# mLSTM stage of a diffusion step: decay and weight rows by transfer, mask by a minimum, two numerator banks, one gate product

## The reference

```python
b = cumsum(log_sigmoid(forget gate)); dmat = where(causal, b_t - b_s + i_s, -inf)
m_t = max(b_t + m, max_s dmat)
s   = (q @ k.T) * exp(dmat - m_t)
num = exp(b + m - m_t) * (q @ C) + s @ v
den = exp(b + m - m_t) * (q @ n) + sum(s)
h   = num / max(|den|, exp(-m_t))
```

## Time and profile before

| | us |
|---|---|
| median of 3 runs | 1567.22 (1565.61 to 1571.27) |
| the profiled execution | 1569.15 |
| its span, first to last instruction | 1567.5 |

### The profile page before, as it was taken

One profiled execution on the slowest core, in us unless ns is written; L12 is line 12 of the kernel. 1 busy time (PEld: TensorE's weight loads), 2 busy tenths in 40 slices (PEclk: granted clock), 3 DMA queues, 4 the chain that ended last, 5 costly groups with the idle time before them and its releaser, 6 DMA issues.

```text
span 1567.5 us, 21088 instructions
## 1 busy us (share of the span) xinstructions
PE 1424.5 (91%) x7059; PEld 1167.0 (74%) x7059; DVE 920.4 (59%) x1259; ACT 733.7 (47%) x1127; POOL 155.9 (10%) x174
## 2 busy tenths in 40 slices
PE   6999888999999899999969879999999999999960
PEld 2766478999999789976638767888888877888750
DVE  1325558433333682216654598555555999999967
ACT  1333545332222433313342466445445888888851
POOL 1000004300000050002200071000000000000013
PEclk9899989999999999989979799999999999999985
DMA  9785652964444245225545399666665999999922
GB/s 329 254 281 178 244 180 72 357 186 131 127 130 121 67 103 140 80 89 184 164 148 170 121 367 374 212 188 198 218 187 182 373 382 375 383 374 374 381 90 86
DMA packets 253682, 336.95 MB, mean 215 GB/s; under 512 B 16670, under 2 KB 210460, under 8 KB 253484
## 3 DMA queue, kind: packets, MB, share of 16 engines
q1 hardware_dynamic: 241210, 299.55, 58.3%
q0 software_dynamic: 11120, 36.43, 6.2%
q10 hardware_dynamic: 1282, 0.04, 0.0%
HBM read 313.41 MB, written 21.50 MB: 214 GB/s over the span
## 4 chain that ended last, share of the span: by engine, by line
PE 81%; DVE 9%; ACT 3%; DMA 3%; issue 3%; SPq 1%; POOL 0%; DVEq 0%; ACTq 0%; POOLq 0%
PE PS L2006 23%; PE PS L479 14%; PE PS L2013 11%; PE PS L468 6%; PE PS L469 6%; PE PS L470 6%; PE PS L598 2%; DVE wlo L1871 2%; DVE wlo L454 1%; PE PS L1356 1%; PE PS L623 1%; PE PS L1981 1%; DMA raw<-in_ada_w 1%; DVE X L773 1%; DVE BIG L768 1%
## 5 line engine op out<-in xcount | busy, mean ns | idle before, releaser
L454 DVE TENSOR_TENSOR wlo<-raw,whi 128x1024 fp32r<-128x1024 f32 x130 | 172.1, 1350 | 252.2 <-ACT whi L451 251.8
L1871 DVE TENSOR_TENSOR wlo<-BIG,whi 128x1024 fp32r<-128x1024 f32 x192 | 238.1, 1256 | 66.6 <-ACT whi L1867 65.2
L1867 ACT ACTIVATE whi<-BIG 128x1024 fp32r<-128x1024 f32 x192 | 202.8, 1060 | 67.5 <-PE PS L2006 40.1
L2006 PE MATMUL PS<-whi,Hh 128*128 128x512 f32 x560 | 223.3, 399 | 2.3 <-DVE Hl L1928 2.2
L1871 DVE TENSOR_TENSOR wlo<-raw,whi 128x1024 fp32r<-128x1024 f32 x150 | 188.2, 1264 | 53.9 <-ACT whi L1867 52.4
L2006 PE MATMUL PS<-whi,Hl 128*128 128x512 f32 x560 | 219.1, 391 | 0.0
L2006 PE MATMUL PS<-wlo,Hh 128*128 128x512 f32 x560 | 218.9, 391 | 0.0
L468 PE MATMUL PS<-Hh,whi 128*128 128x384 f32 x608 | 206.7, 340 | 8.3 <-DVE Hl L758 6.5
L469 PE MATMUL PS<-Hl,whi 128*128 128x384 f32 x608 | 205.1, 337 | 0.0
L470 PE MATMUL PS<-Hh,wlo 128*128 128x384 f32 x608 | 204.9, 337 | 0.0
L1867 ACT ACTIVATE whi<-raw 128x1024 fp32r<-128x1024 f32 x150 | 158.5, 1059 | 70.8 <-PE PS L2013 41.0
(11 more groups left out here) (344 smaller groups left out, 1968.2 us busy)
## 6 DMA issues: line engine op xcount, KB each, us to landing
raw<-in_moe_w_gu SPq DMA_DIRECT2D x224, 256.0 KB, 5.7
BIG<-in_moe_w_gu SPq DMA_DIRECT2D x224, 256.0 KB, 6.0
raw<-in_ada_w SPq DMA_DIRECT2D x96, 512.0 KB, 4.9
BIG<-in_moe_w_down SPq DMA_DIRECT2D x80, 512.0 KB, 7.6
raw<-in_ffn_w_gu SPq DMA_DIRECT2D x44, 512.0 KB, 4.8
raw<-in_w_in_c SPq DMA_DIRECT2D x32, 512.0 KB, 3.9
raw<-in_moe_w_down SPq DMA_DIRECT2D x32, 512.0 KB, 7.3
scr_tok<-BIG POOLq DMA_DIRECT2D x29, 512.0 KB, 9.5
```

The source lines that it names most:

```text
L454: self.eng.tensor_tensor(wlo[:, s, :], raw[:, s, :], whi[:, s, :].bitcast(f32), ALU.subtract).then_inc(lo_made, 1)
L1867: act.activation(whi[:, slot(v), :], moe_raw(v), ACT.Copy).then_inc(hi_made, 1)
L1871: dve.tensor_tensor(wlo[:, slot(v), :], moe_raw(v), whi[:, slot(v), :].bitcast(f32), ALU.subtract).then_inc(lo_made, 1)
L2006: last = pe.matmul(PS[:, 6 * b + c % 2, :], lhs, wt[:, s, 512 * k:512 * k + 512], start=(q == 0 and k == 0 and lhs is h and wt is whi), st ...
```

## The change

The gate weights are put in one tile of 64 columns per block (16 input gates, 16 zeros, 16 forget gates, 16 zeros). Eight products alternate between two halves of the array's columns, and the halves are added on VectorE. In the loop TensorE no longer spreads rows: `negM` and `wint` go to DRAM once, and GpSimd's queue loads each unit's rows into `E` and `qw`, broadcast over 128 partitions. ScalarE's exponents are done in place, VectorE applies the mask by a minimum with 0 or 1, GpSimd multiplies the weight row by q. The numerator alternates between banks 2 and 3, the scores lie in another order, the transposes move to bank 4, the denominator takes two small steps for three, and the modulation units go ahead of the finished head's work.

```diff
-    masks = np.concatenate([np.where(s <= q, 0.0, BIG_NEG), np.where(s >= q, 0.0, BIG_NEG)], 1)
+    masks = np.concatenate([s <= q, s >= q], 1)
...
+        def key_blocks(e, d, key):
+
+            if key == 0:
+                return e[:, 0:128]
+            if key == 1:
+                return e.rearrange("p (a n) -> p a n", a=4)[:, 1::2, :] if d == 0 else e[:, 128:256]
+            return e[:, 256:384] if d == 0 else e[:, 256:512]
+
+        SUMS = ((((0, 0),), ((128, 1),), ((384, 1), (256, 2))),
+                (((0, 0),), ((128, 1), (384, 2)), ((256, 2),)))
...
-            for dst, w in ((4, wgi), (5, wgf)):
-                for k in range(KT):
-                    last = pe.matmul(PS[0:16, dst, 0:T], w[:, k, :], H32[:, k, :], start=(k == 0), stop=(k == KT - 1))
+            for k in range(KT):
+                at = 64 * (k % 2)
+                last = pe.matmul(PS[at:at + 64, 4, 0:T], wgp[:, k, :], H32[:, k, :], start=(k < 2), stop=(k >= KT - 2))
             last.then_inc(gates_mm, 1)
...
+                        st4 = PS[:, 0, :].rearrange("p (a n) -> p a n", a=4)
                         pe.matmul(PS[:, 0, 0:128], kM[:, h, 0:128], qM[:, h, 0:128], start=True, stop=True)
-                        pe.matmul(PS[:, 0, 128:T], kM[:, h, 128:256], qM[:, h, 128:T], start=True, stop=True)
-                        pe.matmul(PS[:, 1, 0:256], kM[:, h, 256:T], qM[:, h, 128:T], start=True, stop=True
+                        pe.matmul(st4[:, 1::2, :], kM[:, h, 128:256],
+                                  qM[:, h, 128:T].rearrange("p (a n) -> p a n", a=2), start=True, stop=True)
+                        pe.matmul(PS[:, 0, 256:384], kM[:, h, 256:T], qM[:, h, 256:T], start=True, stop=True)
+                        pe.matmul(PS[:, 1, 0:128], kM[:, h, 256:T], qM[:, h, 128:256], start=True, stop=True
                                   ).then_inc(st_made, 1)
-                    if i >= 1:
-                        pe.wait_ge(e_made, i)
-                    row = cr[0:16, 0, r:r + 1].to_broadcast([16, 128])
-                    spans = ((0, 384, 0), (384, 512, 256)) if d == 0 else ((0, 256, 0), (256, 512, 128))
-                    for lo, hi, tok in spans:
-                        for part in (nmh, nml):
-                            pe.matmul(PS[:, 2, lo:hi], row, part[:, tok:tok + hi - lo],
-                                      start=(lo == 0 and part is nmh), stop=False, skip_group_check=True)
-                    for lo in (0, 128, 384):
-                        last = pe.matmul(PS[:, 2, lo:lo + 128], cr[:, 0, :], cr[:, 1 + d, :],
-                                         start=False, stop=(lo == 384), skip_group_check=True)
-                    last.then_inc(d_made, 1)
-                    if i >= 1:
-                        pe.wait_ge(qw_made, i)
-                    pe.matmul(PS[:, 4, 0:256], row, wih, start=True, stop=False)
-                    pe.matmul(PS[:, 4, 0:256], row, wil, start=False, stop=True).then_inc(wb_made, 1)
+                        if h >= 2:
+                            pe.wait_ge(ht_made, h - 1)
+                        if h:
+                            pe.wait_ge(kw_made, h)
+                        pe.transpose(PS[:, 4, 0:128], kM[:, h, 0:128], C("ident")).then_inc(km_turned, 1)
                 if 0 <= i - 1 < NM:
                     u = i - 1
                     h, d, r = unit(u)
                     pe.wait_ge(p_done, u + 1)
+                    pe.wait_ge(qw_made, u + 1)
...
-                    if u >= 1:
-                        pe.wait_ge(rd_done, u)
+                    if u >= 2:
+                        pe.wait_ge(rd_done, u - 1)
...
+                        dst = PS[:, 2 + u % 2, 129 * t:129 * t + 129]
+                        for j, (col, key) in enumerate(SUMS[d][t]):
...
-                    if u % 2 == 1:
+                    if u:
                         pe.wait_ge(co_made, u)
-                    if u % 2 == 1 and h >= 1:
-                        pe.wait_ge(ht_made, h)
                     pe.matmul(PS[:, 7, 0:129], kw[:, d, :], V1[:, 0, h, :], start=True, stop=True).then_inc(c_made, 1)
-                if i < NM and i % 2 == 0:
-                    h = i // 2
-                    if h:
-                        pe.wait_ge(co_made, 2 * h)
-                    pe.transpose(PS[:, 7, 0:128], kM[:, h, 0:128], C("ident")).then_inc(km_turned, 1)
+                if i < NM:
+                    ada.units(2)
                 if i >= 3 and i % 2 == 1:
                     h = (i - 3) // 2
                     pe.wait_ge(hn_made, h + 1)
-                    pe.wait_ge(co_made, min(i, NM))
+                    pe.wait_ge(kw_made, min(h + 2, HM))
+                    if h:
+                        pe.wait_ge(ht_made, h)
                     for t in range(TT):
-                        last = pe.transpose(PS[:, 7, 128 * t:128 * t + 128], hn[:, t, :], C("ident"))
+                        last = pe.transpose(PS[:, 4, 128 * t:128 * t + 128], hn[:, t, :], C("ident"))
...
-            ch.step(dve.tensor_scalar(g[1], PS[0:16, 5, 0:T], bgf[:, 0:1], None, ALU.add))
+            ch.step(dve.tensor_scalar(g[1], PS[32:48, 4, 0:T], bgf[:, 0:1], None, ALU.add))
+            ch.step(dve.tensor_tensor(g[1], g[1], PS[96:112, 4, 0:T], ALU.add))
             ch.step(dve.tensor_scalar(g[2], g[1], -1.0, None, ALU.mult))
             dve.tensor_tensor(g[2], g[2], g[1], ALU.min).then_inc(nab_made, 1)
+            dve.wait_ge(gi_made, 1)
+            ch.step(dve.tensor_tensor(g[0], g[0], PS[64:80, 4, 0:T], ALU.add))
...
-                    act.wait_ge(d_made, i + 1)
-                    if i >= 2:
-                        act.wait_ge(num_made, i - 1)
-                    for t, lo, hi in KEYS[d]:
-                        last = act.activation(E[:, i % 2, lo:hi], PS[:, 2, lo:hi], ACT.Exp,
-                                              bias=nat[:, t, r:r + 1])
+                    act.wait_ge(row_in[i % 2], 48 * (i // 2 + 1))
+                    for key in range(3):
+                        e = key_blocks(E[:, i % 2, :], d, key)
+                        last = act.activation(e, e, ACT.Exp, bias=nat[:, key, r:r + 1])
                     last.then_inc(e_made, 1)
...
-                    dve.wait_ge(wb_made, i + 1)
-                    if i >= 2:
-                        dve.wait_ge(num_made, i - 1)
-                    dve.tensor_tensor(qw[:, d, :], PS[:, 4, 0:256], qM[:, h, 128:T], ALU.mult).then_inc(qw_made, 1)
-                    dve.wait_ge(st_made, h + 1)
                     dve.wait_ge(e_made, i + 1)
                     e = E[:, i % 2, :]
+                    e3 = e[:, 0:384].rearrange("p (a n) -> p a n", a=3)
+                    ch.step(dve.tensor_tensor(e3, e3, cr[:, 1 + d, :].bitcast(f32).unsqueeze(1).to_broadcast([128, 3, 128]),
+                                              ALU.min))
+                    dve.wait_ge(st_made, h + 1)
                     if d == 0:
+                        last = dve.tensor_tensor(e, e, PS[:, 0, :], ALU.mult)
+                    else:
                         dve.tensor_tensor(e[:, 0:384], e[:, 0:384], PS[:, 0, 0:384], ALU.mult)
-                        last = dve.tensor_tensor(e[:, 384:512], e[:, 384:512], PS[:, 1, 128:256], ALU.mult)
-                    else:
-                        dve.tensor_tensor(e[:, 0:256], e[:, 0:256], PS[:, 0, 0:256], ALU.mult)
-                        last = dve.tensor_tensor(e[:, 256:512], e[:, 256:512], PS[:, 1, 0:256], ALU.mult)
+                        last = dve.tensor_tensor(e[:, 384:512], e[:, 384:512], PS[:, 1, 0:128], ALU.mult)
                     last.then_inc(p_done, 1)
...
+                    ch.step(dve.tensor_tensor(den, num[:, :, 128:129], nat[:, 3:6, r:r + 1], ALU.max))
+                    ch.step(dve.scalar_tensor_tensor(den, num[:, :, 128:129], -1.0, den, ALU.mult, ALU.max))
                     ch.step(dve.reciprocal(den, den))
...
+                if i < NM:
+                    ada.units(2)
                 if i >= 3 and i % 2 == 1:
                     h = (i - 3) // 2
                     dve.wait_ge(ht_turned, h + 1)
...
+            pool.wait_ge(rows_exp, 2)
+            pool.dma_start(scr["row"][0:16, :], negM).then_inc(row_out, 16)
+            pool.dma_start(scr["row"][16:32, 0:256], wint).then_inc(row_out, 16)
             pool.wait_ge(m_out, 16)
             pool.wait_ge(nat_copied, 1)
-
-            def start_state(u):
+            pool.wait_ge(row_out, 32)
+
+            def start_rows(u):
                 h, d, r = unit(u)
                 if u >= 2:
                     pool.wait_ge(num_made, u - 1)
+                off = 256 if d == 0 else 128
+                pool.dma_start(E[:, u % 2, 0:384], scr["row"][r:r + 1, :].to_broadcast([128, 384])
+                               ).then_inc(row_in[u % 2], 16)
+                pool.dma_start(E[:, u % 2, 384:512], scr["row"][r:r + 1, off:off + 128].to_broadcast([128, 128])
+                               ).then_inc(row_in[u % 2], 16)
```

(27 more changed lines are left out.)

39 lines of the change are left out of this document (7 added, 32 removed).

## The result

The changed kernel takes 1581.04 us (median of 5 runs, 1575.58 to 1587.54) against 1568.33 for the kernel before on the same chip (5 runs): ratio 1.0079, 95% interval 1.0045 to 1.0112. The change makes the kernel slower by 0.8%. The forecast of 1548, faster, is wrong and its range doesn't hold the time. The profiled execution took 1587.54 us, its span is 1585.9, the mean granted clock 0.938 (before 0.955).

The account below looks back on a forecast made before the run. TensorE, 81% of the chain of waits, was taken to bound the kernel, VectorE not far behind. Gates 7.0, first two units 5.0 and later loop 7.2 gave 19.2 us off the 1567.22 median: 1548.0, range 1539 to 1565.

Parts of the forecast that it names:

- Gates: Gate products ahead of the projections: overlapping column halves take 2.6 us for 10.49; gain 7.0 us, bounds 3.0 and 7.9.
- ScalarE's wait for the softplus rows: In the projections: this wait holds back copies of the second and third product, and was said to add no delay.
- R5: Rival in the gate product: column halves run one after the other, 5.25 us; time 1549.8 us, chance 0.03.
- First two units: Start of the mLSTM loop: TensorE drops row, mask and weight-row products; gain 5.0 us, bounds 3 and 6.
- TensorE's and VectorE's lines: Later loop: each engine's own work per pair of units (one head, both directions), 8.2 us for TensorE, 10.6 for VectorE.
- GpSimd's M: In the loop: GpSimd's 128x256 product for one unit, 0.75 us with its start, plus 0.2 for signals.
- L: In the loop: a unit's row transfers from first issue to last landing, taken as 4.5 us, between 3.2 and 6.2.
- part C: The loop after its first two units: 11.3 us a pair; gain 7.2 us, bounds minus 10 and plus 17.
- R1: Rival in the loop: GpSimd's serial line decides, L 5.5 us, 12.9 a pair; time 1558.3 us, chance 0.18.
- R2: Rival in the loop: TensorE's clock falls to 1.2 GHz, a pair takes it 16.4 us; time 1581, slower, chance 0.11.
- R4: Rival in the loop: GpSimd's product and VectorE contend for SBUF, costing 6.5 us; time 1554.5 us, chance 0.10.
- R3: Rival in the loop: all waits hidden, L under 4, VectorE at 10.3 us a pair; time 1537 us, chance 0.10.

Follow-up runs that it names:

- e8_all: The change with one row transfer per unit from 128 copies in DRAM, four row buffers, weight-row product on VectorE: 1547.52 us, ratio 0.9857.
- e3_quiet: The change with the modulation units moved out of the loop to behind it, so no weights stream beside the rows: 1594.17 us, a single run.
- e4_dvemul: The change with the weight-row product on VectorE instead of GpSimd, still two buffers: 1576.78 us, ratio 1.0056.
- e9_all_pool: The kernel of e8_all with the weight-row product back on GpSimd: 1545.34 us, ratio 0.9847.
- e10_ahead: The kernel of e9_all_pool with ScalarE doing its exponents one unit ahead: 1539.34 us, ratio 0.9790.
- e12_actq: The kernel of e4_dvemul with the three row transfers issued from ScalarE's queue instead of GpSimd's: 1584.57 us, ratio 1.0091.

## Why the prediction was wrong

- **Gates, 7.0 forecast: 5.6 in the trace, 4.0 in the medians.** Product (2.80 for 2.6) and weight split (580.35) were right. The step "ScalarE's wait for the softplus rows ... falls in the same gap" failed: it stood ahead of the fourth product for 1.79 us, behind VectorE's L1396, and the eighth was no longer the one that waited. R5 is out.
- **First two units, 5.0: 8.2.** Right in kind. The second scores come 6.0 us after the first for 14.2; the price was read from TensorE's broadcasts alone, and what hung on them went too.
- **TensorE's and VectorE's lines, 8.2 and 10.6 a pair:** VectorE's is borne out. With the rows out of the way the pair is 10.9 (with 0.84 us more on VectorE), 10.5 and 10.2. TensorE's has no such test: it is busy 8.6 us a pair in e8_all, gate broadcasts included.
- **GpSimd's M, 0.75 + 0.2:** 0.64, right.
- **L, "I take 4.5, near the middle", between 3.2 and 6.2: this is the step that failed.** It is 7.5, above the end of my range (7.0 over the stretch of the pairs). By my own formula, 7.5 + 0.65 a unit would give 16.3 a pair; measured 17.1. I bounded it with single transfers beside a stream that left the engines 43% idle, and asked of three broadcasts only how many bytes they bring. What counted was the time for which they hold the engines: 39% of it, with 7.2 MB. Beside them the states land in 6.5 us for 2.1 and the weights in 7.4 for 4.4; without the weights the rows' L is 5.6 (e3_quiet).
- **"bounds minus 10 ... and plus 17" for part C:** it came to -30, of which 6.2 lie behind the last scores, where I had written that the loop's end stays. R1 was the right place at a wrong size: I let L end at 5.5 there because the states' 2.1 us spoke against more. The states were at 6.5 themselves once the rows ran beside them. R1 also named GpSimd's serial order. Taking that away alone is worth 0.9, because the closed loop of two buffers stands right behind it: numerator of unit u-2, rows, exponents, minimum, product, scores, numerator of u. I left this loop out. From the parts in e4_dvemul it is L + 7.9 at the lower clock and some L + 5.7 at the higher one: at L = 4.5 that is 10.2 at the higher clock, just under VectorE's line, and 12.4 at the lower one, above it; at 8.2, e4_dvemul's own L, it is the 16.1 measured. Four buffers take 4.4 us out of the pair of the change.
- **R2, the clock:** its sign (1.2 GHz in parts of the loop, 0.77) came true, its time (1581) too, by chance. Fillers that raise the clock to 0.89 give nothing back.
- **R4, contention for SBUF, 6.5 us:** no part of it shows in the change's loop, where it was priced. In the gates it does (L1396, 2.65 us, the wait above), and in e9_all_pool and e10_ahead, where GpSimd's product meets VectorE's sum, that sum grows from 0.56 us to medians of 0.82 and 1.01.
- **R3, all hidden, 1537:** what e10_ahead reaches (1539.34) once three things are added that the change lacks: rows brought in one transfer from own copies, four buffers, and exponents ahead.

The Trainium skill ("DMA: Bandwidth & Descriptors", the section on the anatomy of a SWDGE DMA) gave 3.4 to 4.0 us for L by 2.0 us and bytes over 436 GB/s, an estimate; for one transfer of 192, 64 or 128 KB the same rule gives 2.2 to 2.5. The trace doesn't agree: landings were 4.2, 4.7 and 6.4 us. They don't follow the size: the third of a unit's three transfers lands last, and without the weights beside them they land in 4.0, 4.5 and 4.5 (e3_quiet).

## What to carry to other kernels

A transfer that takes a product's place on the critical engine is priced by the time for which it holds the 16 engines, and that is read from a queue's share, not from its bytes; bring what one step needs in one transfer, laid out beforehand as the buffer wants it. With two buffers the whole latency (issue, landing, and every step until the buffer is free again) is a loop of its own, to be summed beside the engines' lines, at the clock that TensorE will have when it waits. A landing read from a quiet stretch is no upper bound for one in a stretch that the change itself will fill.

## What the runs showed of the hardware that I had not expected

- 384 KB read from one DRAM row by 128 partitions in three transfers hold the 16 engines for about 2.8 us in the change (3.3 with the states' 0.5), and for 2.2 to 3.1 in the other runs that do the same; from own copies 1.0; in one transfer from one row 1.4.
- Issued by ScalarE, the 128 KB rows land in 7.1 us, by GpSimd in 7.3 (e12_actq, e4_dvemul).
- A sum of VectorE over 128x384 with both inputs in SBUF takes 0.56 us alone and up to 1.71 where GpSimd's 128x256 product falls beside it (from 766.49 and 767.04 in e10_ahead); the product itself takes 0.63 us (median) in the change and 0.64 to 0.73 in e9_all_pool.
- In e3_quiet, with TensorE at the lowest clock of all (0.76), the pair is 2.6 us shorter than in the change, though with less work in it: the mean clock of a stretch says little of the time where TensorE mostly waits.
